# Two expert products side by side in the two column tiles of TensorE, weights of gate and up in 1 MB transfers

## What is computed

```
x_slots = xf[slot_tok].reshape(n_blocks, MOE_BLOCK, d)

def expert_block(args):
    xb, e = args
    return (jax.nn.silu(xb @ w_gate[e]) * (xb @ w_up[e])) @ w_down[e]

y_slots = lax.map(expert_block, (x_slots, block_expert)).reshape(cap, d)
y_assign = y_slots[dest] * g_sorted[:, None].astype(h.dtype)
y = jax.ops.segment_sum(y_assign, tok_sorted, num_segments=t)
```

## Time and profile before

| | |
|---|---|
| median of 3 runs | 1877.78 us (1877.2 to 1879.83) |
| the profiled execution | 1880.45 us, span 1878.6 us |
| mean granted TensorE clock | 0.991 |
| busy share of the span | PE 96%, PEld 62%, DVE 46%, ACT 41%, POOL 6% |
| mean DMA rate over the span | 292 GB/s |
| first experts stage | about 849 to 1306 us of the span |
| second experts stage | about 1424 to 1870 us of the span |
| jobs in the two stages | 32 and 31 (32 matmul records of L1941 each) |
| in the first stage | the chain of waits runs through PE to 1072 us, then through the transfers of down |

### The profile page before, as it was taken

One profiled execution on the slowest core, in us unless ns is written; L12 is line 12 of the kernel. 1 busy time (PEld: TensorE's weight loads), 2 busy tenths in 40 slices (PEclk: granted clock), 3 DMA queues, 4 the chain that ended last, 5 costly groups with the idle time before them and its releaser, 6 DMA issues.

```text
span 1878.6 us, 27537 instructions
## 1 busy us (share of the span) xinstructions
PE 1809.1 (96%) x10423; PEld 1168.1 (62%) x10423; DVE 856.5 (46%) x1595; ACT 771.3 (41%) x1394; POOL 105.6 (6%) x148
## 2 busy tenths in 40 slices
PE   8999999998999999999999999999999999999997
PEld 6779998886799998974344333335975334333334
DVE  4766656678765556874121111114785121211113
ACT  5554334556543335533333333334543333333333
POOL 3420000112200000010000000000010000000000
PEclk9999999998999999999999999999998999999999
DMA  9545555552355644459999999999548999999995
GB/s 328 198 160 192 190 180 179 167 167 70 100 184 180 197 159 156 157 224 398 421 429 426 427 425 428 429 428 347 202 180 344 414 428 428 426 426 429 429 429 217
DMA packets 130594, 549.42 MB, mean 292 GB/s; under 512 B 8030, under 2 KB 67768, under 8 KB 103480
## 3 DMA queue, kind: packets, MB, share of 16 engines
q1 hardware_dynamic: 127080, 539.53, 73.2%
q0 software_dynamic: 3088, 8.10, 1.3%
q10 hardware_dynamic: 320, 0.34, 0.1%
HBM read 546.83 MB, written 1.11 MB: 292 GB/s over the span
## 4 chain that ended last, share of the span: by engine, by line
PE 76%; DMA 16%; DVE 4%; ACT 1%; POOL 1%; issue 1%; SPq 0%; POOLq 0%; DVEq 0%; ACTq 0%
PE pb L1379 28%; DMA raw<-in_w_expert_down 16%; PE pb L1941 14%; PE pb L1970 11%; PE pb L1674 6%; PE pb L1949 3%; PE pb L1959 2%; PE pb L1508 1%; PE pb L1531 1%; PE pb L1608 1%; PE pb L1485 1%; POOL rms L902 1%; DVE parts L2133 1%; PE pb L1391 1%; PE pb L2041 1%
## 5 line engine op out<-in xcount | busy, mean ns | idle before, releaser
L2133 DVE TENSOR_TENSOR parts<-raw,parts 128x2048 fp32r<-128x2048 f32 (+1 forms) x138 | 307.2, 2232 | 108.1 <-ACT parts L922 105.1
L922 ACT ACTIVATE parts<-raw 128x2048 fp32r<-128x2048 f32 (+1 forms) x138 | 256.6, 1867 | 209.6 <-PE pb L1379 153.1
L1379 PE MATMUL pb<-xT,parts 128*128 128x256 f32 (+1 forms) x2712 | 333.3, 283 | 0.0
L1379 PEld LDWEIGHTS pb<-xT,parts 128*128 128x128 f32 (+1 forms) x2712 | 329.2, 191 | 4.7 <-issue 2.9
L1941 PE MATMUL pb<-raw,xw 128*64 128x512 f32 x1360 | 319.5, 601 | 11.0 <-DMA raw<-in_w_expert_gate 11.0
L2753 DVE TENSOR_TENSOR qk<-qk,pb 128x256 f32<-128x256 f32 x126 | 53.1, 421 | 548.3 <-ACT qk L1234 548.1
L1379 PE MATMUL pb<-parts,xT 128*128 128x512 f32 (+1 forms) x1200 | 272.0, 385 | 2.6 <-DVE xT L2144 1.5
L1379 PEld LDWEIGHTS pb<-parts,xT 128*128 128x128 f32 x1200 | 217.8, 189 | 48.7 <-issue 3.9
L1941 PEld LDWEIGHTS pb<-raw,xw 128*64 128x64 f32 x1360 | 86.6, 136 | 153.2 <-issue 129.7
L1970 PE MATMUL pb<-raw,qk 128*64 128x512 f32 x624 | 142.8, 596 | 19.8 <-DMA raw<-in_w_expert_down 19.8
L1229 ACT ACTIVATE qk<-pb 128x512 f32<-128x512 f32 x126 | 74.9, 595 | 178.2 <-PE pb L1941 178.2
(11 more groups left out here) (336 smaller groups left out, 1676.6 us busy)
## 6 DMA issues: line engine op xcount, KB each, us to landing
raw<-in_w_expert_gate SPq DMA_DIRECT2D x41, 2048.0 KB, 10.0
raw<-in_w_expert_up SPq DMA_DIRECT2D x37, 2048.0 KB, 10.4
raw<-in_w_expert_down SPq DMA_DIRECT2D x35, 2048.0 KB, 10.7
spare<-in_w_expert_down SPq DMA_DIRECT2D x16, 2048.0 KB, 15.1
spare<-in_w_expert_up SPq DMA_DIRECT2D x14, 2048.0 KB, 13.1
raw<-in_w_ffn_gate SPq DMA_DIRECT2D x22, 1024.0 KB, 5.4
raw<-in_w_ffn_up SPq DMA_DIRECT2D x22, 1024.0 KB, 5.3
raw<-in_w_ffn_down SPq DMA_DIRECT2D x22, 1024.0 KB, 4.9
```

The costliest lines, as they stand in the source:

```text
L922: nc.scalar.activation(parts[:, (SPL0[seg] + k) % SPL, 0, 0:kk * nn], raw[:, place, 0:kk * nn], ACT.Copy).then_inc(hi_done[seg], 1)
L1379: ins = mm(out_ap, b if flip else a, a if flip else b, start=first and n == 0, stop=last and n == 2)
L2133: v.tensor_tensor(two[:, 1, :], raw[:, place, 0:kk * nn], two[:, 0, :].bitcast(F32), ALU.subtract)\
```

## The change

**Products.** Gate now goes to PSUM partitions 0 to 63 and up to partitions 64 to 127 of one bank, for the same `k` and the same stationary operand. Each accumulates over all eight `k`, so nothing has to be added afterwards. One copy, one set of four transposes and no sums are left; the tanh and the two products of the hidden part read PSUM directly. Down puts its output columns 0 to 511 on the first tile and 512 to 1023 on the second, with one copy, four transposes and one copy into the slots. The number of matmuls is unchanged.

**Weights.** PE now needs gate and up of the same half of `k` together. A unit of gate and up is therefore "gate half beside up half", two transfers of 1 MB with 8 KB per partition. Down stays at 2 MB. The homes and their order, by `plan`, stay as they were, and a unit waits for `used` as before.

```diff
-                    for k in range(4):
-                        rows = slice(W * (k % 2), W * (k % 2 + 1))
-                        ins = mm(pb[m][rows, :], xw[:, 4 * hf + k, :], w[:, k, :], start=(hf == 0 and k < 2),
-                                 stop=(hf == 1 and k >= 2))
-                    ins.then_inc(used[seg], 1)
+                    for k in range(4):
+                        for m in range(2):
+                            ins = mm(pb[0][W * m:W * (m + 1), :], xw[:, 4 * hf + k, :], w[m][:, k, :],
+                                     start=(hf == 0 and k == 0), stop=(hf == 1 and k == 3))
+                            if k == 3:
+                                ins.then_inc(used[seg], 1)
...
-                    pe.wait_ge(yadd_done[l], at(j, 2, 1 - 2 * back))
-                    for b in range(2):
-                        pe.wait_ge(ys_done[l], at(j, 2, b + 1 - 2 * back))
-                        for q in range(4):
-                            ins = nc.tensor.transpose(pb[6 + b][:, P * q:P * (q + 1)], ys[:, 512 * b + P * q:512 * b + P * (q + 1)],
-                                                      ident)
-                        ins.then_inc(yt2_ready[l], 1)
+                    pe.wait_ge(yadd_done[l], at(j, 1, 1 - back))
+                    pe.wait_ge(ys_done[l], at(j, 1, 1 - back))
+                    for q in range(4):
+                        ins = nc.tensor.transpose(pb[6][:, P * q:P * (q + 1)], ys[:, P * q:P * (q + 1)], ident)
+                    ins.then_inc(yt2_ready[l], 1)
...
-                        for c in range(2):
-                            for k in range(2):
-                                ins = mm(pb[4 + c][W * k:W * (k + 1), :], ehj[:, 2 * hf + k, :],
-                                         w[:, k, 512 * c:512 * (c + 1)], start=(hf == 0), stop=(hf == 1))
+                        for k in range(2):
+                            for c in range(2):
+                                ins = mm(pb[4][W * c:W * (c + 1), :], ehj[:, 2 * hf + k, :],
+                                         w[:, k, 512 * c:512 * (c + 1)], start=(hf == 0 and k == 0),
+                                         stop=(hf == 1 and k == 1))
...
+            def load_halves(l, j, e, q, half):
+
+                sp.wait_ge(used[2 * l + 1], home_free(j, q + 1))
+                _, there, _ = job_home(l, j, q)
+                place = (RAW0[2 * l + 1] + q - 2) % RAW
+                for m in range(2):
+                    sp.dma_start(raw[:, place + m, :].rearrange("p (k n) -> p k n", k=4),
+                                 weights(l, m, e)[:, 4 * half:4 * half + 4, :]).then_inc(there, 16)
...
-                        first_parts(j, 1, 0, eg)
-                        first_parts(j, 1, 1, eu)
                         tanh(j, 1)
-                    if later:
-                        to_slots(j, 2)
-                    products(j, gs, gs_done, 0, g1)
-                    products(j, us, us_done, 1, u1)
+                    act.wait_ge(used[seg], at(j, 6, gate_up(j)[1][0]))
+                    nc.scalar.activation(gs, pb[0][:], ACT.Copy).then_inc(gs_done[l], 1)
```

More of the change, by code:

```diff
@@ L401, in put @@
                 kind, x = where[0]
+                pieces = len(where) if i < 4 else 1
                 if kind == "raw":
@@ L474, in gate_up @@
             q0 = 2 if isinstance(j, int) and j == 0 else 0
-            return [(q0 + 2 * m + hf, m, hf) for m in range(2) for hf in range(2)]
+            return [(q0 + 2 * hf, hf) for hf in range(2)]
         def down_at(last):
@@ L490, in job_home @@
             first = place - place % 2
-            return raw[:, place, :], arrived[2 * l + 1][first], at(j, 16, 16 * (PLAN[l][2][first] - FIXED))
+            per_job = 16 if q >= 4 else 32
+            return raw[:, place, :], arrived[2 * l + 1][first], at(j, per_job, 16 * PLAN[l][2][first] - per_job * FIXED - 16 * last)
         def last_half(l):
@@ L742, in load_fixed @@
                 job, i, n, home, there, waits = unit
-                m, half = i // 2, i % 2
                 for one in waits:
                     sp.wait_ge(*one)
+                if i < 4:
+                    for x in range(n):
+                        m, half = (i + x) % 2, (i + x) // 2
+                        sp.dma_start(home[:, x, :].rearrange("p (k n) -> p k n", k=4),
+                                     weights(l, m, e)[:, 4 * half:4 * half + 4, :]).then_inc(there, 16)
+                    return
+                m, half = 2, i - 4
                 k = SHAPES[m][0] // 2
@@ L748, in load_fixed, with load_down @@
                              weights(l, m, e)[:, k * half:k * (half + n), :]).then_inc(there, 16)
-            def load_job(l, j, e, q, m, last=False):
+            def load_halves(l, j, e, q, half):
[4 more added lines that the diff above has]
+                    sp.dma_start(raw[:, place + m, :].rearrange("p (k n) -> p k n", k=4),
+                                 weights(l, m, e)[:, 4 * half:4 * half + 4, :]).then_inc(there, 16)
+            def load_down(l, j, e, q, last=False):
+                m = 2
                 sp.wait_ge(used[2 * l + 1], home_free(j, q + 1))
@@ L776, in gate_up_of @@
                 def gate_up_of(j, e):
-                    for q, m, hf in gate_up(j):
-                        if hf == 0:
-                            load_job(l, j, e, q, m)
+                    for q, half in gate_up(j):
+                        load_halves(l, j, e, q, half)
                 def down_of(j, e, last=False):
-                    load_job(l, j, e, down_at(last), 2, last)
+                    load_down(l, j, e, down_at(last), last)
                 units = PLAN[l][0]
@@ L1927, in landed @@
                 def landed(j, q, shape, last=False):
-                    home, there, count = job_home(l, j, q)
+                    home, there, count = job_home(l, j, q, last)
                     if last and q % 2:
@@ L1989, in step @@
                     pe.wait_ge(xw_ready[l], at(j, 1, 0))
[L1990 removed]
+                    turn(j, 1)
                     products(j, *halves[0])
[L1992 to L1995 removed]
                     if fixed == GATES_AT + 1:
@@ L2028, in moe @@
                 end = (more, 1)
-                turn(end, 1, 0, gs, gs_done)
-                turn(end, 1, 1, us, us_done)
+                turn(end, 1)
                 down(more, 1, down_at(False), range(1, 2))
@@ L2813, in moe @@
                 low_slots(1)
-                sums(end, 1)
                 hidden(end, 1, at(more, 6, 4))
```

102 lines of the change are left out of this document (35 added, 67 removed).

## The result

The changed kernel takes 1884.1 us (median of 11 runs, 1879.82 to 1885.39) against 1878.32 us for the kernel before in 11 runs beside it. The ratio is 1.0020 with an interval of 1.0012 to 1.0029, so 3.8 us (2.3 to 5.4) are lost. In a later series it came to 1.0014 (1.0006 to 1.0023), or 2.6 us. The forecast was 4.2 us more.

The account below looks back on a forecast made before the run. The prediction took the experts stages to be bound by DMA bytes, with PE hidden. Packets at +8.1 us and layer ends at -3.9 us gave +4.2 us on 1877.8, so 1882.0 us, range 1875.5 to 1887 for 8 in 10.

Parts of the forecast that it names:

- The bound and PE's cover: Experts stages: DMA bounds them at 14.69 us a job, hiding PE's fall from 13.13 to about 11.8 us.
- at zero: Experts stages: the work saved per job on PE, ACT and DVE was costed at nothing; uncovered, 1.35 us per job.
- The transfers: Gate and up loads: 8 KB in place of 16 KB packets cost 8.1 us more, ends 2.4 and 12.2.
- 0.078 us per pair: Gate and up loads: extra time per 2 MB pair moved as 1 MB units, over 104 pairs.
- The head: Stage start at the routing table: later release of homes costs 0, with 0.5 us a layer as upper end.
- the 1.7 forecast: Stage start: PE's first released home comes 1.7 us later, after 16 matmuls and not 8.
- The end of a layer: Behind each layer's last landings: PE's shorter work saves 1.9 us a layer, 3.9 us for two.
- 8 KB packets cost nothing: Rival on gate and up transfers: only the layer ends count, giving 1873.9 us; chance 0.12.
- PE bounds the stage: Rival on the early part of the experts stages: 43 us would go, giving 1835 us; chance 0.04.
- the transfers starve or PE slows: Rival in the experts stages: late issues or a lower clock; 0.2 us per job gives 1894 us; chance 0.10.
- The sum of 4.2 us: Whole kernel: net loss of 4.2 us, giving 1882.0 us; its case, the byte price wins, had chance 0.74.
- Its two terms: Whole kernel: 8.1 us more for smaller packets and 3.9 us less at the ends of two layers.

Follow-up runs that it names:

- fifth: Kernel before, with only a quarter of down's weights loaded and read, by as many matmuls; 1867.55 us, one run.
- sixth: Changed kernel, with only a quarter of down's weights loaded and read, by as many matmuls; 1802.51 us, one run.
- seventh run: Kernel before with the down part of the change alone, all transfers as before; 1875.7 us, ratio 0.9979; repeated, 1875.94 us, ratio 0.9975.
- first experiment: Kernel before, with each 2 MB transfer of gate or up issued as two of 1 MB, one per half of k; 1887.91 us, ratio 1.0043.
- eighth: Kernel before, gate and up still in 2 MB transfers, but halves of k in swapped homes, so 8 KB pieces; 1886.55 us, ratio 1.0036.
- ninth: Changed kernel with its down part taken back; gate beside up and the 1 MB transfers stay; 1885.08 us, ratio 1.0026 to the kernel before.
- fourth run: Changed kernel, with gate and up in whole 2 MB transfers for jobs 0 to 16; 1885.08 us, ratio 1.0032 to the kernel before.
- second run: Kernel before, with each 2 MB gate or up transfer split into partitions 0 to 63 and 64 to 127; 2599.1 us, ratio 1.3776.

## Why the prediction was right

**The bound and PE's cover.** DMA stayed full and 1.26 us less of PE per job moved nothing late in the stage. The fifth and sixth runs show that the cover hid a real saving. One statement there was too strong: that PE's time per job drops out of the sum altogether. In the stage's first 80 us the homes are all in use and PE's releases set SP's issues, so a slower PE leaves holes in the transfers. That is some 0.9 us a layer of the seventh run, which "at zero" left out. The gain is in the changed kernel too: its four stages lack the hole of 76 to 80 us that its transfers have with PE's order of before (first and eighth experiments).

**The transfers.** Forecast 8.1 us, measured 8.1 by ratio and 7.6 in the stages (first experiment), 6.8 and 6.3 in the eighth. The forecast of 0.078 us per pair is 0.07 in the steady rows: (14.83 - 14.69)/2, and 104 x 0.07 = 7.3 us. So the size is right to about 1 us, and that the 8.1 came again to the digit is luck. The eighth run, with the number of transfers unchanged, settles that it is the packet. The rule of the Trainium skill (DMA: Bandwidth & Descriptors, Specifications), line rate from 512 B up, does not hold here to the last per cent: 16 KB packets give 428 GB/s and 8 KB ones 423 to 424. What inside the DMA engines takes the extra time stays open.

**The head.** Taken as 0, with 0.5 us a layer as the upper end. In the changed kernel's second layer, SP and then two windows of 8 us:

```profile
1421.27 0.35 SPq L758 DMA_DIRECT2D extra<-in_w_expert_gate  x1
...
1429.45 0.33 SPq L758 DMA_DIRECT2D raw<-in_w_expert_up  x1
```

```profile
1429.27:1437.27 8.00, 8.00 (x44) 4.76 (x42) 7.09 (x11) 2.67 (x5) 0.00 (x0) 1.00 0.99 384
1437.27:1445.27 8.00, 8.00 (x41) 3.76 (x38) 0.96 (x3) 1.18 (x2) 0.00 (x0) 1.00 0.99 395
```

The first released home came 8.18 us behind the table's first issue, beyond the 7.3 us that were queued; in the kernel before it was 6.62 (from 1419.79 to 1426.41). The two windows lose about 0.75 + 0.55 = 1.3 us against 424; the kernel before lost 0.8 us in the first of them (382 GB/s). But both of these stages began with PE's clock low (0.75 and 0.77 in their first 4 us), which delays the release too. In the stages that began at 1.00 it came at 4.86 us before and at 6.39, 6.87 and 6.69 us in the changed kernel and its repeat, 1.5 to 2.0 us later for the 1.7 forecast. In the first of these three the rate held at 426 and 419 (8 us each); in the other two it fell to 386 and 398 GB/s in the first 8 us, which is 0.8 and 0.5 us, though the release came before the 7.3 us were over. So the step was right in its delay and low in its price: the queue ran short in three of the four stages, for 0.5 to 1.3 us, where the forecast had 0 and at most 0.5.

**The end of a layer.** Forecast 1.9 us. From the start of the third last down to the addition into `h` it was 32.22 us and is 1308.83 - 1278.27 = 30.56; 1.66 us less, and 1.7 in the second layer. With 0.15 us that the longer period takes inside this stretch it is 1.8. The last down starts at 1299.06, 5.99 us behind the landing of the down ahead of it (1293.07); in the kernel before it was 1295.72 - 1288.25 = 7.47. That is 1.5 us nearer, as forecast.

**The rivals.** That 8 KB packets cost nothing fell with the late rate of 423 to 424 GB/s. That PE bounds the stage fell with the period. That the transfers starve or PE slows came true in small: at the table in three of four stages, and at the hand-over to the loop in one of four, where the clock fell to 0.95 in 32 us and 1.3 us went. In the steady loop the clock was 1.00 at 82 us of 100 busy. The sum of 4.2 us stood against 3.8 and 2.6 measured. Its two terms measured one by one are 7.3 us for 8.1 and 3.3 to 3.6 for 3.9, both a little smaller and of opposite sign. It left out two small terms, the holes and the short queue at the table, which have opposite signs as well. So the mechanism was right, and that the sum came within 0.4 us (1.6 in the repeat) is partly luck.

**What stays open.** The parts don't add up exactly by ratio: the down part gains 3.9 and 4.7 us on the kernel before, but only 1 to 2 us on top of the ninth. Part of it is that either half of the change alone removes the same hole of 76 to 80 us (422 and 424 GB/s there in the ninth run, 430 to 438 in the seventh and its repeat), so it can't be gained twice. The intervals of about 2 us leave room for no difference at all. Open too is why PE's clock falls in one run of a kernel and not in the next.

## What to carry to other kernels

In these stages, bound by their bytes, work taken from an engine was worth only what stood behind the last byte and what brought releases forward at the stage's start, while a layout that cut transfers smaller was paid for on every byte. So split a change into its parts and time each: here the half that touches no transfer (down's output halves side by side) makes the kernel 0.2% faster, and the whole makes it 0.2% slower. A DMA share of 1.00 is no proof of a full queue; look at the GB/s of short windows and at the time from issue to landing. And before a difference between two single traces is put down to a change, look whether both stages began at the same clock.

## What the runs showed of the hardware

**Transfers to 64 partitions.** With gate and up in transfers of 1 MB to 64 partitions, issued in turn for both halves, the stage moved 223 GB/s with the DMA engines busy throughout, against 428 for 128 partitions. The Trainium skill (SBUF — State Buffer, Door 1: The DMA port swizzle) says that partitions 0 to 63 reach only half of the 16 ports; half of the 435 GB/s that the Trainium skill (DMA: Bandwidth & Descriptors, Specifications) gives for all of them is 218 as an estimate, and the run's 223 is near it. It is no clean reading of one half, since a third of the bytes was down's, in 128 partitions. What it shows plainly is that with both halves in the queue in turn the full rate was not reached.

**What a packet costs.** 8 KB for 16 KB packets cost 0.07 us per 2 MB pair, with 8 more packets on each of 16 engines: about 9 ns each, as an estimate.

**PE's clock and how waits are spread.** From 1100 to 1200 us, at 82 us of 100 busy in three short waits a job (0.7, 0.7 and 1.2 us), the granted clock was 1.00. In the fourth run, at 86 to 87 of 100 busy, it was 0.97 and 0.93, and the waits just ahead of a fall were of 1.84, 2.75 and 2.74 us, while one of 2.63 us had none behind it. At the hand-over the changed kernel waited once 2.27 us and stayed at 1.00, and in its repeat 2.13 us and fell to 0.70 in the 5 us behind. In the second run, at 66 of 100 busy, the clock was 0.81.
